# A two-model kernel on one core: the order of its first loads and steps, and the work split at four turns between sublayers

## The reference

```python
sc = jax.nn.silu(c)
for i in range(DEPTH):                                     # 2 layers
    mod = (sc @ ada_w[i] + ada_b[i]).reshape(B, N_MOD, D_MODEL)
    # feed-forward, then a mixer (pooling / latent attention), then feed-forward, each by:
def modulated_sublayer(x, mod, g_pre, g_post, fn, weight):
    shift, scale, gate = mod[:, 0], mod[:, 1], mod[:, 2]
    h = rmsnorm(x, g_pre) * (1.0 + scale) + shift
    y = rmsnorm(fn(h), g_post)
    return x + weight * (1.0 + gate) * y
def swiglu(h, w_in, w_out):
    gate, up = jnp.split(h @ w_in, 2, axis=-1)
    return (jax.nn.silu(gate) * up) @ w_out                # 1024 -> 2 x 2816 -> 1024
```

## Time and profile before

| | |
|---|---|
| median of 3 runs (lowest, highest) | 1566.01 us (1565.28, 1566.88) |
| the profiled execution: its time, its span | 1568.05 us, 1565.8 us |
| busy share of the span: PE, DVE, ACT, POOL | 97%, 78%, 56%, 7% |
| share of the chain that ended last: PE, ACT, DVE, DMA | 88%, 4%, 4%, 1% |
| bytes moved by DMA, mean rate | 373.75 MB, 239 GB/s |
| granted clock of PE, mean over the span | 0.993 |

### The profile page before, as it was taken

One profiled execution on the slowest core, in us unless ns is written; L12 is line 12 of the kernel. 1 busy time (PEld: TensorE's weight loads), 2 busy tenths in 40 slices (PEclk: granted clock), 3 DMA queues, 4 the chain that ended last, 5 costly groups with the idle time before them and its releaser, 6 DMA issues.

```text
span 1565.8 us, 19135 instructions
## 1 busy us (share of the span) xinstructions
PE 1520.5 (97%) x7373; PEld 1213.7 (78%) x7373; DVE 1214.8 (78%) x1774; ACT 882.1 (56%) x1357; POOL 115.5 (7%) x176
## 2 busy tenths in 40 slices
PE   6999999999999999999999999999999999999998
PEld 3878876887877887776788887777788888787876
DVE  1898978888867888655586654669888798988996
ACT  3545436544437444476564544655567477776774
POOL 1110020000002000015211000000001000000000
PEclk9999999999999999999999999899999999999999
DMA  9999856998857988333287544445323469989993
GB/s 345 373 378 348 303 206 213 319 315 294 308 173 268 327 295 298 136 109 108 82 295 203 167 163 135 163 143 194 113 89 124 168 248 359 348 315 327 324 338 134
DMA packets 196401, 373.75 MB, mean 239 GB/s; under 512 B 9042, under 2 KB 102672, under 8 KB 196304
## 3 DMA queue, kind: packets, MB, share of 16 engines
q1 hardware_dynamic: 176688, 301.08, 55.7%
q0 software_dynamic: 18928, 69.77, 12.7%
q10 hardware_dynamic: 688, 1.62, 0.3%
HBM read 371.39 MB, written 1.05 MB: 238 GB/s over the span
## 4 chain that ended last, share of the span: by engine, by line
PE 88%; ACT 4%; DVE 4%; DMA 1%; POOL 1%; issue 1%; SPq 0%; DVEq 0%; ACTq 0%
PE banks L524 26%; PE banks L526 25%; PE banks L525 25%; PE banks L1124 1%; ACT arena L802 1%; DVE ul L460 1%; ACT uh L449 1%; PE banks L2361 1%; DMA raw<-in_ffn_w_in 1%; PE banks L2963 1%; PE banks L1970 1%; PE banks L761 1%; ACT full L1038 1%; DMA raw<-in_ada_w 1%; PE banks L1795 1%
## 5 line engine op out<-in xcount | busy, mean ns | idle before, releaser
L460 DVE TENSOR_TENSOR ul<-raw,uh 128x1024 fp32r<-128x1024 f32 (+2 forms) x548 | 656.9, 1209 | 148.9 <-ACT uh L449 139.7
L449 ACT ACTIVATE uh<-raw 128x1024 fp32r<-128x1024 f32 (+2 forms) x548 | 568.4, 1048 | 347.8 <-PE banks L526 341.6
L524 PE MATMUL banks<-uh,hh 128*128 128x512 f32 (+2 forms) x1296 | 517.7, 399 | 13.0 <-DVE hl L1069 6.4
L526 PE MATMUL banks<-uh,hl 128*128 128x512 f32 (+2 forms) x1296 | 504.7, 389 | 0.0
L525 PE MATMUL banks<-ul,hh 128*128 128x512 f32 (+2 forms) x1296 | 503.2, 388 | 0.0
L524 PEld LDWEIGHTS banks<-uh,hh 128*128 128x128 f32 x1296 | 244.8, 189 | 72.2 <-DVE hl L1069 10.1
L526 PEld LDWEIGHTS banks<-uh,hl 128*128 128x128 f32 x1296 | 244.8, 189 | 51.4
L525 PEld LDWEIGHTS banks<-ul,hh 128*128 128x128 f32 x1296 | 245.3, 189 | 45.8 <-issue 0.2
L524 PE MATMUL banks<-uh,bh 128*128 128x512 f32 x512 | 207.2, 405 | 1.0 <-DVE bl L3160 0.9
L526 PE MATMUL banks<-uh,bl 128*128 128x512 f32 x512 | 200.1, 391 | 0.0
L525 PE MATMUL banks<-ul,bh 128*128 128x512 f32 x512 | 199.6, 390 | 0.0
(11 more groups left out here) (392 smaller groups left out, 1270.8 us busy)
## 6 DMA issues: line engine op xcount, KB each, us to landing
raw<-in_ffn_w_in SPq DMA_DIRECT2D x176, 512.0 KB, 6.6
raw<-in_w_up SPq DMA_DIRECT2D x64, 1024.0 KB, 7.1
arena<-in_ada_w POOLq DMA_DIRECT2D x60, 1024.0 KB, 6.6
raw<-in_ffn_w_out SPq DMA_DIRECT2D x44, 1024.0 KB, 5.5
raw<-in_w_down SPq DMA_DIRECT2D x32, 1024.0 KB, 7.0
raw<-in_w_in SPq DMA_DIRECT2D x22, 1024.0 KB, 5.0
raw<-in_ada_w SPq DMA_DIRECT2D x12, 1024.0 KB, 11.0
raw<-in_w_mem_kv SPq DMA_DIRECT2D x4, 1024.0 KB, 6.5
```

The lines of the kernel that those rows point to most:

```text
L449: act.e.activation(uh[r][:, 0:w], raw[m % NRAW][:, h * w:(h + 1) * w], AF.Copy).then_inc(act_done, ta.put("hi", u))
L460: dve.e.tensor_tensor(ul[r][:, 0:w], raw[m % NRAW][:, h * w:(h + 1) * w], uh[r][:, 0:w].bitcast(F32), ALU.subtract).then_inc(dve_done, tv. ...
L524: pe.e.matmul(o, a, wh, start=k + j == s0, stop=False)
L526: mm = pe.e.matmul(o, b, wh, start=False, stop=k + j == s1)
```

## The change

In the opening, the first chunk of feed-forward weights is loaded after two pieces of modulation and no longer after three. ACT splits its first unit between the copies of pieces one and two, and DVE its low part before it writes scale and shift. PE adds both first biases ahead of everything, turns the first four blocks before the products of the two pieces, sums both pieces, and then turns the rest. Pieces three and four come together after the first unit's matmuls, then their two sums, then the second unit; the six fillers are gone. The roots of x are made by POOL (one addition and one power for each tile), and ACT's square root with its table loads is gone.

At the four turns, tile 0's first pair goes block by block: ACT scales block 0, writes its high part, scales block 1, writes its high part; DVE has a low part for each, and PE waits for each block. The second pair of tile 0 is scaled by DVE from PSUM (`second_scaled`) and only its high part is ACT's. ACT does pair 2 ahead of `x_squares(1)`, DVE does the scaling and the low parts of blocks 0 and 1 and of pair 1 ahead of `update(1)`. `bias` and `scale` are passed to `edge_dve` for that.

```diff
-    for a in ADA_FIRST[:3]:
+    for a in ADA_FIRST[:2]:
...
-    ffn(0, 0, ADA_FIRST[3:])
+    ffn(0, 0, ADA_FIRST[2:])
...
-        def ada_parts_pe(pe, a, b):
-            i, j = a
-            r = i * 18 + j
-            got = [take_raw(pe, ("ada", i, j)) for _ in range(2)]
+        def ada_bias_pe(pe, a, b):
+            r = a[0] * 18 + a[1]
...
+        def ada_products_pe(pe, a, b):
+            got = [take_raw(pe, ("ada",) + a) for _ in range(2)]
...
+        def ada_parts_pe(pe, a, b):
+            ada_bias_pe(pe, a, b)
+            ada_products_pe(pe, a, b)
...
-                pe.frees(b, act_done, ta, "tf", q, t, g)
+                if (t, g) == (0, 1):
+                    pe.frees(b, dve_done, tv, "tf", q, 0, 1)
+                else:
+                    pe.frees(b, act_done, ta, "tf", q, t, g)
...
-            return lambda k, t: pe.wait_ge(dve_done, tv("tl", q, t, k // 2))
+            return lambda k, t: pe.wait_ge(dve_done, tv("first", q, k) if (t, k // 2) == (0, 0) else
+                                           tv("tl", q, t, k // 2))
...
+            def first_high():
+                act.wait_ge(pe_done, tp("T", q, 0, 0))
+                for k in range(2):
+                    v = edge_part(0, 0)[:, k, :]
+                    act.e.activation(v, PB[EDGE_BANKS[0]][:, k * P:(k + 1) * P], AF.Identity, bias=bias(k),
+                                     scale=scale(k)).then_inc(act_done, ta.put())
+                    if k:
+                        ta.same("tf", q, 0, 0)
+                    act.own()
+                    act.e.activation(hh[:, k, 0:P], v, AF.Copy).then_inc(act_done, ta.put("first", q, k))
+            def second_high():
+                act.wait_ge(dve_done, tv("tf", q, 0, 1))
+                act.e.activation(edge_columns(hh, 0, 1), edge_part(0, 1), AF.Copy).then_inc(
+                    act_done, ta.put("th", q, 0, 1))
...
-                if t:
+                if t and g == 0:
+                    act.wait_ge(dve_done, tv("first", q, 1))
+                elif t:
...
-            high(0, 0)
-            high(0, 1)
+            first_high()
+            second_high()
+            high(0, 2)
...
-            high(0, 2)
...
-        def edge_dve(dve, s, q, key, more=True):
+        def edge_dve(dve, s, q, key, scale, bias, more=True):
             def low(t, g):
...
+            def first_low():
+                for k in range(2):
+                    dve.wait_ge(act_done, ta("first", q, k))
+                    dve.e.tensor_tensor(hl[:, k, 0:P], edge_part(0, 0)[:, k, :], hh[:, k, 0:P].bitcast(F32),
+                                        ALU.subtract).then_inc(dve_done, tv.put("first", q, k))
+            def second_scaled():
+                dve.wait_ge(pe_done, tp("T", q, 0, 1))
+                for k in range(2):
+                    dve.e.tensor_scalar(edge_part(0, 1)[:, k, :], PB[EDGE_BANKS[1]][:, k * P:(k + 1) * P], scale(2 + k),
+                                        bias(2 + k), ALU.mult, ALU.add).then_inc(dve_done, tv.put())
+                tv.same("tf", q, 0, 1)
...
-            low(0, 0)
+            second_scaled()
+            first_low()
+            low(0, 1)
...
-            low(0, 1)
+            low(0, 2)
...
-            low(0, 2)
...
-            ada_parts_pe(pe, first[0], 2)
+            ada_bias_pe(pe, first[0], 2)
+            ada_bias_pe(pe, first[1], 3)
...
+            ada_products_pe(pe, first[0], 2)
+            ada_products_pe(pe, first[1], 3)
...
-            ada_parts_pe(pe, first[1], 3)
...
-            ada_parts_pe(pe, first[2], 2)
...
+            ada_parts_pe(pe, first[2], 2)
...
-            first_parts(*got[1], 2, 0)
...
-            first_parts(*got[1], 2, 1).then_inc(pe_done, tp.put("used", got[1][0]))
-            keep_busy(pe, 4, 6)
+            for t in range(T):
+                mm = first_parts(*got[1], 2, t)
+            mm.then_inc(pe_done, tp.put("used", got[1][0]))
...
         def start_act(act):
...
-            diag_act(act, 0, lambda t: act.wait_ge(loaded(f"x{t}"), 16), junk=x_junk)
-            act.wait_ge(loaded("sum4"), 16)
-            silu_table_act(act)
+            for t in range(T):
+                act.wait_ge(loaded(f"x{t}"), 16)
+                squares_act(act, st[:, 4 + t:5 + t], x[:, t, :], "xsq", 0, t, junk=x_junk, scale=D ** -0.5)
...
+            split_high(act, act.unit_at)
...
-            ada_skip(act, ADA_FIRST[2])
-            split_high(act, act.unit_at)
...
-            ada_copy_act(act, ADA_FIRST[2], 2, START_BUFS[2])
+            piece(2)
...
-            diag_dve(dve, 0)
+            for t in range(T):
+                dve.wait_ge(pool_done, tg("xr", 0, t))
+                dve.e.tensor_scalar(dgx[t], ident[:, :], st[:, 6 + t:7 + t], None, ALU.mult).then_inc(
+                    dve_done, tv.put("dg", 0, t))
...
-            for n in range(3):
+            for n in range(2):
...
+            split_low(dve, dve.unit_at)
...
-            ada_skip(dve, ADA_FIRST[3])
+            for n in (2, 3):
+                ada_skip(dve, ADA_FIRST[n])
...
-                    edge_dve(dve, 5, "mix", ("pj",))
+                    edge_dve(dve, 5, "mix", ("pj",), lambda k: col("g_mix_2", k), lambda k: 0.0)
...
-            pool.wait_ge(act_done, ta("xsq", 0, 1))
+            for t in range(T):
+                r = st[:, 6 + t:7 + t]
+                pool.wait_ge(act_done, ta("xsq", 0, t))
+                pool.wait_ge(pool_done, tg.n)
+                pool.e.tensor_scalar(r, st[:, 4 + t:5 + t], EPS, None, ALU.add).then_inc(pool_done, tg.put())
+                pool.wait_ge(pool_done, tg.n)
+                pool.e.tensor_tensor(r, r, minus_half, ALU.pow).then_inc(pool_done, tg.put("xr", 0, t))
...
```

More of the change, by code:

```diff
@@ L1283, in sub_ffn_dve @@
             else:
-                edge_dve(dve, q - 1, q, up_key(i, s)(0))
+                edge_dve(dve, q - 1, q, up_key(i, s)(0), *modulated(q))
             ffn_dve(dve, q, NFF, up_key(i, s), down_key(i, s), side, tail=tail, begun=q != 2, edge=q > 0)
@@ L2041, in mla_dve @@
         def mla_dve(dve):
-            edge_dve(dve, 3, 4, ("mi",), more=False)
+            edge_dve(dve, 3, 4, ("mi",), *modulated(4), more=False)
             for t in range(T):
```

## The result

| | before | after |
|---|---|---|
| median, 19 runs each (lowest, highest) | 1566.15 us (1563.46, 1569.73) | 1563.76 us (1561.36, 1565.62) |
| ratio after to before, 95% interval | | 0.9981 (0.9973 to 0.9989) |
| the profiled execution: time, span | 1568.05, 1565.8 us | 1564.39, 1562.3 us |
| granted clock, mean | 0.993 | 0.990 |

The change saves 2.4 us by the medians (3.7 between the two profiled executions), where 4.7 were forecast. It is faster by 0.19%, clear of the noise by its interval, and inside the 3.1 us that the prediction called "within" and gave 0.26.

The account below looks back on a forecast made before the run. TensorE's stream of products and its standstills were taken to bound the kernel. The opening's 3.4 us and the turns' 1.3 sum to 4.7, taking the median from 1566.01 to 1561.3 us; range 1558.5 to 1564.5.

Parts of the forecast that it names:

- within: Whole kernel: a difference from before of no more than 3.1 us, given chance 0.26.
- The opening: Kernel start: first product at 26.7, second half of the inputs at 40.3 instead of 43.69, a gain of 3.4 us.
- rival (a): Opening: a stretch of half clock falls on the new chain and costs 1.7 us, giving 1563.0; chance 0.15.
- from the end of the sums to the first product I take 2.6: Opening: 2.6 us from the second piece's sums to the first product, putting that product at 26.7.
- They end earlier, and the bout may be over by 26.7: Opening: argument against lower clock on the new chain, that idle stretches and half clock end before the first product.
- The turns: Four turns between sublayers: gains of 0.6 twice, 0.3 and -0.2, together 1.3 us, bounds -0.8 to 3.0.
- `update(1)` starts at about 478.8 instead of 478.01: Turns: DVE's added work delays tile 1's update, so its diagonal comes at 482.9 instead of 482.14.
- rival (c): Turns: a later update(1) and diagonal hold up TensorE; 2.5 us later loses 5.5, giving 1568.1; chance 0.04.
- The upper bound of 3.0: Turns: most the four could gain together, 3.0 us, if update(1) comes only 0.3 later.
- (b): Opening: transfers set the pace, so it gives nothing and only the turns remain, giving 1564.7; chance 0.11.
- (d): Opening: TensorE's chain is shorter, transfers bind at 38.9, and the turns give 2.4, giving 1558.8; chance 0.06.
- (e): Opening: POOL's root comes late, each microsecond of lateness from 16.6 on costing one; chance 0.02.

Follow-up runs that it names:

- e3: The whole change plus fifteen unread filler matmuls in TensorE's two idle stretches of the opening: 1561.59 us, ratio 0.9969 to the kernel before.
- e2: The kernel before with only the new turns, the opening as before: 1564.15 us, ratio 0.9988 to the kernel before.
- e1: The kernel before with only the new opening, the turns as before: 1565.24 us, ratio 0.9992 to the kernel before.
- e8: e3 with the first pair at the turns whole again, only the second pair scaled by DVE with its order: 1560.02 us, ratio 0.9966 to before.
- e4: The whole change, but ACT copies piece two before the first weight split and DVE's split follows the scaling: 1561.54 us, ratio 0.9964 to before.
- e5: e4 plus filler matmuls in TensorE's three remaining holes of the opening: 1560.34 us, ratio 0.9964 to the kernel before.
- e10: e8 with DVE's second-half low part before its weight splits, ten fillers replaced by turning the last four blocks: 1564.15 us, ratio 0.9987 to before.

## Why the prediction was right and wrong

**The number.** 1563.76 lies in the stated range (1558.5 to 1564.5), near its upper end and 2.5 above the likeliest value. The prediction gave 0.70 to a gain over 3.1 us, and that didn't come. The two terms missed in opposite directions, 2.4 too much for the opening and 1.1 too little for the turns, and that their sum was no further off is luck.

**The opening, 3.4 us forecast, 0.96 measured: mis-sized, by rival (a).** Every number up to the copy was right: the weights at 21.67 (21.5), the copy, the roots at 9.7 (well before 16.6), no later wait for a transfer. The step that failed is "from the end of the sums to the first product I take 2.6", with sums of 0.95, at full clock. Against the forecast of 26.7 the first product is 1.9 late. Of that e3 shows 0.56 to be the chain itself (27.26 with the clock up: sums from 23.52 and not 23.16, and 2.8 from their end to the first product), and the other 1.35 to be the clock, since turning at half clock takes 3.76 and becomes longer than the chain beside it. The twelve products and two pieces then took 9.07 (28.61 to 37.68) instead of 8.6, their start still being in the bout; with the clock up e3 has 8.58, the forecast to 0.02. The last stretch is 5.05 for 4.96. Sum of the misses: 1.91 + 0.47 + 0.09 = 2.47, against 42.73 - 40.3 = 2.43; the rest is rounding.

The rival itself was priced at 1.7 us and given 0.15. The price was near (1.83 between the change and e3); the chance was too low. "They end earlier, and the bout may be over by 26.7" had no row behind it; the bout lasted from 22.8 to about 29.7. What the rows did show was an idle stretch of 3.03 us with half clock after it, and the forecast's own numbers held another: the chunk ahead of the weights lands at 21.5 - 2.7 = 18.8, half a piece (1.0) and the first sums (1.0) end at 20.8, and the second sums wait for the copy until 21.5 + 1.06 + 0.60 = 23.2. That hole of 2.4 us in front of the chain was there to be worked out.

**The base.** 43.69 was taken as the kernel's number, but e2's trace of the same opening has 41.99. Against that the change's opening, with its bout, is 0.7 us behind, and e3's is 1.1 ahead; e1, the same opening as the change, has 41.86. So the same opening moves by 0.9 to 1.7 us between two traces, and the 0.96 is one such difference. The medians give the opening 1.2 us (e1, interval -0.2 to 2.7). By the mean granted clocks above the new opening meets a bout as a rule; how often the old one does is left open.

**The turns, 1.3 us forecast, 2.4 measured: mis-sized the other way.** The first product 2.18 behind the turning (forecast 2.2), blocks of 0.31 and 0.29 us on ACT and DVE (0.32 and 0.30). DVE's scaling of 128 columns from PSUM:

```profile
L1108 DVE TENSOR_SCALAR full<-banks,ab x6: 401/405/410, 474.0 to 777.4; 128x128 f32<-128x128 f32 x6
```

405 ns for the 0.41 taken as the middle of 0.28 and 0.54. The estimate from the Trainium skill, VectorE: DVE Perf Modes, section "The TRN2 errata" (120 cycles plus one for each column), is 0.26; the row doesn't agree with it. What failed is "`update(1)` starts at about 478.8 instead of 478.01", 0.8 later: it was 3.26 - 2.72 = 0.54 later, and the diagonal 0.42 (6.99 behind the turning, 6.57 before), since part of DVE's added work fell into its waits for ACT, as rival (c) had said. Tile 1's turning came 7.33 behind tile 0's and not 7.6. The last turn, forecast to lose 0.2, gained 0.3, though with bouts of different length in the two traces. The upper bound of 3.0 was added up wrongly: with `update(1)` later by 0.3 its rooms of 1.37, 1.37, 1.11 and 0.57 leave 3.2.

**Rival (c)'s mechanism is there.** In all four turns TensorE now stands in front of the second turning until the diagonal comes, 0.61, 0.67, 0.61 and 1.08 us. Those 3.0 us are given back out of what the earlier first product and pairs had won. The forecast's own sum had it so ("turning starts at 482.9", when the diagonal is there), and e8 shows that without the blocks each of the first three turns would be 0.2 us shorter.

**Rivals (b), (d) and (e)** didn't occur in the change: ACT waits once for a transfer, 3.92 us; (d)'s transfer bound shows only in e4. POOL's first sum runs at 7.19, right after ACT's squares, and each root takes 0.9. Nothing of the 6 us that the Trainium skill, GPSIMD Engine Reference, section "2. Architecture", gives for the first call to a freshly loaded kernel is seen here either.

## What to carry to other kernels

- When steps are moved in a stretch where TensorE isn't full, write down its idle stretches after the move, not only the chain. Here those of 2.7 us and more in the opening were followed by half clock, which cost about 2 us when needed work came next, wherever it had been moved to. Shorter ones are not safe: half clock followed on 1.44 us in e4.
- Blocks finer than a pair only help where the first block is what is waited for. Find what ends the stretch instead: here first ACT's second and third pair, and, once work was taken off ACT, the update of tile 1 on DVE. Each part of a change deserves its own run: one of the two here was worth nothing.
- The change with fillers in the opening and without the blocks is 0.34% below the kernel before (1560.02 us). The runs don't tell it from e3 (0.31%), e4 or e5 (0.36% each).

## What the runs showed of the hardware

Half clock followed on idle stretches of TensorE of 3.03 us (before), 2.73 (after and e1) and 2.77 (e10); after 1.69 (e2) and 0.87 (e3) in the same part of the program it stayed at full. But the length of the wait doesn't decide alone: half clock followed on 1.44 us in e4, and the wait of 1.87 or 1.88 us near 272 was followed by it in five traces of twelve, the clock being at its upper level before the wait in all twelve. In the change and in e10 the lower clock is granted while TensorE is still idle, so the first instruction after the hole is already slow: 1.86 us for sums that take 0.95.

In the last turn tile 1 was turned in 3.78 us in the change, 3.45 in e8 and 3.64 before: half clock, in a stretch of 72-column products with waits between. Fillers in the opening don't touch it, and it was not tried to fill that one. Some bout lies between 970 and 990 in all twelve traces.
